# The last quarter of the final layer norm's scale and shift, moved from VectorE to GpSimd

## The reference

```python
def layer_norm(x, g, b):
    mu = jnp.mean(xf, axis=-1, keepdims=True)
    xc = xf - mu
    var = jnp.mean(xc * xc, axis=-1, keepdims=True)
    y = xc * lax.rsqrt(var + LN_EPS) * g + b
...
    x = layer_norm(DEEPNORM_ALPHA * x + y, ln_g[layer], ln_b[layer])
```

## Time and profile before

| | before |
|---|---|
| time, median of 3 runs | 3601.96 us (3601.51 to 3603.68) |
| profiled execution's span, first to last instruction | 3601.3 us |
| TensorE's last product, as the chain of waits has it | ends at 3582.83 us |
| VectorE's sixteen instructions of `ln_last` | 3586.78 to 3598.11 us |
| output issues | 4 of 512 KB, 2.8 us from issue to landing |

### The profile page before, as it was taken

One profiled execution on the slowest core, in us unless ns is written; L12 is line 12 of the kernel. 1 busy time (PEld: TensorE's weight loads), 2 busy tenths in 40 slices (PEclk: granted clock), 3 DMA queues, 4 the chain that ended last, 5 costly groups with the idle time before them and its releaser, 6 DMA issues.

```text
span 3601.3 us, 38810 instructions
## 1 busy us (share of the span) xinstructions
PE 3244.4 (90%) x13642; PEld 2303.8 (64%) x13642; DVE 1733.7 (48%) x2546; ACT 1336.4 (37%) x2042; POOL 2214.8 (61%) x1228
## 2 busy tenths in 40 slices
PE   9999999995787788777777789999999999999998
PEld 7888878883343334222322338888888888878886
DVE  7998264217666447544744552222232123435443
ACT  6776575452111001000100014444444444445653
POOL 2021767887544544555555537887788778878666
PEclk9999999997999999999999999999999999999999
DMA  7455545658999999999999985555555555555444
GB/s 229 137 151 138 170 148 161 222 176 340 419 419 420 422 419 421 421 420 422 420 416 422 419 346 195 175 172 172 169 173 174 170 168 177 172 180 177 146 145 163
DMA packets 232700, 936.78 MB, mean 260 GB/s; under 512 B 28112, under 2 KB 31184, under 8 KB 165968
## 3 DMA queue, kind: packets, MB, share of 16 engines
q0 software_dynamic: 76288, 538.74, 36.2%
q1 hardware_dynamic: 152784, 391.96, 34.3%
q10 hardware_dynamic: 3456, 3.77, 0.3%
HBM read 927.04 MB, written 2.10 MB: 258 GB/s over the span
## 4 chain that ended last, share of the span: by engine, by line
PE 54%; DMA 25%; POOL 10%; issue 5%; DVE 4%; ACT 1%; DVEq 0%; ACTq 0%; POOLq 0%; SPq 0%
PE products L665 32%; DMA arena<-peer_up_in,arena 20%; POOL weights_low L627 8%; PE products L1984 7%; PE products L1339 7%; DMA arena<-peer_down_in,arena 4%; POOL arena L1929 2%; DVE arena L1938 1%; PE products L1070 1%; PE products L2545 1%; PE products L2507 1%; PE products L1176 1%; PE products L1093 1%; PE products L1313 0%; PE products L1082 0%
## 5 line engine op out<-in xcount | busy, mean ns | idle before, releaser
L627 POOL TENSOR_TENSOR weights_low<-arena,weights_high 128x1024 fp32r<-128x1024 f32 x492 | 1208.8, 2465 | 366.2 <-ACT weights_high L615 333.4
L1984 PE MATMUL products<-arena 128*128 128x512 f32 x1984 | 940.8, 619 | 312.8 <-DMA arena<-peer_up_in,arena 230.5
L615 ACT ACTIVATE weights_high<-arena 128x1024 fp32r<-128x1024 f32 x612 | 646.3, 1059 | 991.5 <-PE products L665 965.0
L665 PE MATMUL products<-weights_high,input_high 128*128 128x512 f32 x2432 | 989.4, 407 | 1.9 <-DVE input_low L641 0.8
L665 PE MATMUL products<-weights_low,input_high 128*128 128x512 f32 x2432 | 951.2, 391 | 0.0
L665 PE MATMUL products<-weights_high,input_low 128*128 128x512 f32 x2432 | 948.9, 390 | 0.0
L1984 PEld LDWEIGHTS products<-arena 128*128 128x128 f32 x1984 | 370.3, 195 | 864.5 <-issue 453.2
L1938 DVE SCALAR_TENSOR_TENSOR arena<-arena 128x2048 f32<-128x2048 f32 x256 | 586.0, 2292 | 523.2 <-DMA arena<-peer_down_in,arena 522.8
L1929 POOL DMA_INDIRECT arena<-peer_up_in,arena x256 | 386.7, 1511 | 521.6 <-PE products L1984 497.1
L665 PEld LDWEIGHTS products<-weights_high,input_high 128*128 128x128 f32 x2432 | 457.8, 188 | 97.5 <-issue 8.0
L665 PEld LDWEIGHTS products<-weights_low,input_high 128*128 128x128 f32 x2432 | 456.8, 188 | 98.9
(11 more groups left out here) (339 smaller groups left out, 2999.4 us busy)
## 6 DMA issues: line engine op xcount, KB each, us to landing
arena<-dsa_in SPq DMA_DIRECT2D x320, 512.0 KB, 3.5
arena<-w_in_in SPq DMA_DIRECT2D x128, 512.0 KB, 4.0
arena<-mla_wide_in SPq DMA_DIRECT2D x88, 512.0 KB, 3.5
arena<-w_attn_o_in SPq DMA_DIRECT2D x32, 512.0 KB, 4.4
arena<-w_out_in SPq DMA_DIRECT2D x32, 512.0 KB, 4.7
arena<-peer_w_query_in SPq DMA_DIRECT2D x32, 512.0 KB, 4.6
arena<-dsa_w_out_in SPq DMA_DIRECT2D x32, 512.0 KB, 3.8
arena<-glu_w_b_in SPq DMA_DIRECT2D x16, 512.0 KB, 3.7
```

Source lines behind the costliest of these rows:

```text
L615: nc.scalar.activation(w_hi[:, u % RING, :, at], ring[:, u % RING, :, at], ACT.Copy).then_inc(hi_made, 1)
L627: ops.tensor_tensor(w_lo[:, u % RING, :, at], ring[:, u % RING, :, at], w_hi[:, u % RING, :, at].bitcast(F32), op=ALU.subtract).then_inc(l ...
L665: mm = nc.tensor.matmul(PS[:, bank(b) + t, 0:width], x[:, x0 + n, at], y, start=n == 0 and m == 0, stop=n == len(parts) * PK - 1 and m == 2)
L1984: mm = nc.tensor.matmul(PS[:, SUM_BANKS[q]], diag[:, d % ROWS], row[:, q * NC:(q + 1) * NC], start=h % 2 == 0 and n == 0, stop=bool(last))
```

## The change

The loop of `ln_last` goes over three quarters instead of four. The fourth is made by GpSimd in a new function behind its last `mla_lo`, with two instructions that subtract the mean and multiply by the reciprocal, a drain, two that multiply by the gain, a drain, and two that add the shift. A new semaphore, `inverse_ready`, is raised by VectorE behind `ln_inverse`; GpSimd waits for it and for the gain and shift (`ln_in`). Another, `quarter_done`, is what SyncE waits for before the fourth output.

```diff
         def ln_last(dve):
             dve.wait_ge(ln_in, 64)
-            for q in range(4):
+            for q in range(3):
...
+        def ln_last_quarter(pool):
+
+            at = slice(3 * NC, 4 * NC)
+            pool.wait_ge(ln_in, 64)
+            pool.wait_ge(inverse_ready, 1)
+            for t in range(NT):
+                nc.gpsimd.tensor_scalar(X[:, t, at], X[:, t, at], ln_moments[:, t, 0:1], full_inv[:, t:t + 1],
+                                        ALU.subtract, ALU.mult)
+            pool.drain()
+            for t in range(NT):
+                nc.gpsimd.tensor_tensor(X[:, t, at], X[:, t, at], last_gain[:, at], op=ALU.mult)
+            pool.drain()
+            for t in range(NT):
+                last = nc.gpsimd.tensor_tensor(X[:, t, at], X[:, t, at], last_shift[:, at], op=ALU.add)
+            last.then_inc(quarter_done, 1)
...
-                sp.wait_ge(ln_done, PARTS + q + 1)
+                if q < 3:
+                    sp.wait_ge(ln_done, PARTS + q + 1)
+                else:
+                    sp.wait_ge(quarter_done, 1)
...
             for n in range(len(M_ORDER)):
                 mla_lo(pool, n)
+            ln_last_quarter(pool)
...
             ln_inverse(dve, 1)
+            dve.sem_inc(inverse_ready, 1)
             ln_last(dve)
```

More of the change, by code:

```diff
@@ L581, in program @@
         normal_high, tile_made = sem("normal_high"), sem("tile_made")
+        inverse_ready, quarter_done = sem("inverse_ready"), sem("quarter_done")
         apart = {"dve": sem("apart_dve"), "pe": sem("apart_pe"), "pool": sem("apart_pool")}
```

## The result

The changed kernel takes 3609.84 us (median of 11 runs, 3607.53 to 3612.17), the kernel before 3602.31 us on the same chip (11 runs, 3599.67 to 3603.82): 1.0021 times as long, interval 1.0013 to 1.0028, or 7.5 us more. I had forecast 4.2 us more, as 3606 us. The time lies just inside the range, and 7.5 us are barely more than the 7.2 us that I had called measurable; but they are not made of the terms of my sum.

A forecast was written before the change was run, and what follows sets the result against it. Bound by VectorE's stream in series with one output DMA, the last stage was to give 3595.30 + 5.4 + 0.1 + 1.5 + 3.19 = 3605.5 us, 4.2 more than before: forecast 3606 us, range 3600.5 to 3610.

The forecast's parts named there:

- with two drains some 6.8: GpSimd's fourth quarter: its six instructions alone take 6.6 us, with two drains some 6.8, done by 3593.7.
- which nothing waits for: GpSimd's end, about 3596.3 in alternation with VectorE, holds nothing up: its output stands behind VectorE's third on SyncE's queue.
- 0.80 us from the copy: GpSimd's tensor_scalar of 512 columns, priced by scaling its 252-column copy of 396 ns; ends 0.53 and 2.66 us.
- the tensor_scalar is dear: Rival at GpSimd's fourth quarter: tensor_scalar costs more than a copy; at 2.66 us each, time 3609.8 us; chance 0.07.
- the signs that I had named: In the changed profile: VectorE's first six or so 1.2 to 2 us, third output near 3600.7, first tensor_scalar within 0.2 us.
- The 5.4 us of delay to VectorE: In `ln_last`, GpSimd's six instructions delay VectorE's three quarters by 4 x 1.05 + 2 x 0.60 us, to 3600.7.
- My 0.60 us for each tensor_scalar: In `ln_last`, each GpSimd tensor_scalar delays VectorE by 0.60 us, a pair taking 0.80 + 0.46 = 1.26.
- the four times 1.05: In `ln_last`, each of GpSimd's four two-input instructions delays VectorE by 1.05 us, a pair taking 1.71.
- the alternation of the earlier trace: Around 3270 us, VectorE's `finish_rows` and GpSimd's subtractions run in turn, 1.83 and 1.85 us each.
- The rule of the Trainium skill that I weighed: Two-SBUF-input VectorE and SBUF-reading GpSimd instructions hold shared ports for whole lengths: 7.1 us of delay, time near 3607.8.
- The 1.5 us for two outputs that stand together: At the end, the third and fourth outputs' packets follow each other: 1.5 us more than one output's tail.
- the late reload: Rival on GpSimd ahead of its fourth quarter: library reload takes the whole 36.8 us, time 3624.4 us; chance 0.08.

The follow-up runs named there:

- three quarters only: The changed kernel with the fourth quarter's scale and shift left out, GpSimd only raising `quarter_done`: 3600.15 us, 0.9994 of the kernel before.
- the early drain: The changed kernel with one more GpSimd drain, right behind its last subtraction and ahead of the library reload: 3604.36 us, 1.0005 of the kernel before.
- the two kernels of the last experiment: The changed kernel with a drain behind the row fetches and the last shift's load issued by GpSimd, as one DMA or 32: 3603.38 and 3621.95 us.

## Why the time lay in the range, and where the prediction's reasons failed

**The step that failed** is the one that gave GpSimd's stream "with two drains some 6.8" us, and the sentence built on it, that GpSimd's end is one "which nothing waits for". I had counted two drains at 0.1 us each, and at nothing in the end at 3596.3, with no row for one on GpSimd and no bound from above. The first took 7.3 us more than the work in front of it. It is the price of GpSimd's DMA issues, moved by the edit from the end of the program, where VectorE's stage hid it, into the chain. The runs show it three times over: moved to idle time it costs nothing there (the loss falls from 7.5 to 2.2 us), left out it returns at the program's end, and it comes and goes with the DMAs issued.

**The tensor_scalar was mis-sized.** I took 0.80 us from the copy between ends of 0.53 and 2.66; it is 2.09 alone, inside the ends but far from my value, and 3.09 beside VectorE, where my way gave 0.80 + 0.46 = 1.26. My rival "the tensor_scalar is dear" gave 3609.8 us, all but the time measured, but for another reason: it had VectorE delayed by 9.1 us, and VectorE ended earlier than in the forecast.

**That the time lies in the range is luck.** The forecast had VectorE last, at 3600.7 - 3586.7 = 14.0 us behind the reciprocal, and GpSimd done at 9.6; measured, VectorE was done at 9.1 and GpSimd came last, at 18.9. Of the signs that I had named, only the start of the first tensor_scalar came (0.22 us behind the reciprocal); VectorE's first instructions did not last 1.2 to 2 us, and the fourth output did wait for GpSimd. A delay of VectorE that did not come and a drain that I had all but left out led, by two different paths, to ends of the span within 4 us of each other, and the range's upper end came from the dear tensor_scalar, which would have lengthened the time by another path.

GpSimd's end, from the forecast's 9.6 us behind the reciprocal to 18.9: 6.19 - 2 x 1.26 = 3.7 us for the tensor_scalars, 7.5 for the drains, less 4 x 1.71 - 2 x 2.48 = 1.9 for two-input instructions that ran alone.

**The ports.** The 5.4 us of delay to VectorE were 9.12 - 8.65 = 0.5 us in the changed kernel (8.65 with three quarters only), because ten of VectorE's twelve instructions ran at 0.74 to 0.75 us, those beside the tensor_scalars too but for two (0.94 and 1.02, in the merged rows of 1.60 and 1.68 us), and the two-input ones came too late to meet it. My 0.60 us for each tensor_scalar was thus too much, and the four times 1.05 were right in kind: with the early drain the alternation of the earlier trace rows came, a pair every 1.6 us where I had 1.71, and VectorE lost 12.0 - 9.1 = 2.9 us. These fell on three of its instructions, of 1.60 to 1.75 us instead of 0.74: 0.95 each, so near my 1.05 where the two really meet. The rule of the Trainium skill that I weighed ("SBUF — State Buffer", section "Who interferes with whom"), whole instructions in turn, doesn't fit the tensor_scalars: VectorE finished four of its instructions while one of GpSimd's went on.

**The output's tail.** The 1.5 us for two outputs that stand together are right where they do: 1.4 us with three quarters only. In the changed kernel the fourth came 9.8 us after the third, so the term was nothing, and from GpSimd's end to the span's end are 22.1 - 18.9 = 3.2 us, as taken over from before.

**What held.** The raise of `inverse_ready` costs nothing to speak of (the first of `ln_last` starts 0.12 us behind the reciprocal, 0.09 before). The reload is hidden, and the late reload with it is out: the first tensor_scalar starts 0.22 us behind the reciprocal. With the early drain the reload could begin only behind it, at 3582.95, and the tensor_scalar still started at 3585.55, so it takes at most 2.6 us here; the 6 us of the Trainium skill ("GPSIMD Engine Reference", section 2.1) aren't seen, and the first tensor_scalar lasts 3.12 us, the second 3.07. A quarter is worth 2.8 us of VectorE, but only 1.4 us of the span, since the outputs then queue.

## What to carry to other kernels

Where an engine gets new work at its end, look at what that engine's final drain did before: if it outlasts the last instruction by microseconds, as here by 7.3, a drain that the edit puts on the path may have to pay for it, and a drain put earlier into idle time took it away here. Before work moves from VectorE to GpSimd, see whether VectorE reads a second input from SBUF at that time: here the 2.8 us taken off VectorE came back as 3.3 us of delay (12.0 with the early drain against 8.7 with three quarters only), until that input lay in PSUM. And at a kernel's tail the order in which outputs become ready is part of the sum: a free helper for a quarter brought 1.4 us of 2.8, until its output went ahead of the last one.

## What the runs showed of the hardware that I had not expected

A drain on GpSimd costs some 0.08 us for each DMA that GpSimd itself has issued since its last drain (1, 32 and 80 plain DMAs: 0.1, 2.6 and 6.6 us), 7.3 us behind 512 indirect ones, and that they have landed long before, or that the engine has been idle for 10 us, doesn't spare it. With transfers under way it lasts longer, to 4.1 us behind the last packet of the fetches. Between 80 and 512 no run was made, so where the upper end lies is open, and what the drain does in that time too.

On GpSimd a tensor_scalar with two operations is dearer (2.1 us for 512 columns) than a two-input product (1.25), and in the changed kernel it left VectorE nearly undisturbed but was itself drawn out by half, to 3.1 us. These are no fixed prices: in the two kernels of the last experiment, where VectorE's first instruction starts 0.20 us behind the reciprocal instead of 0.13, the tensor_scalars take 2.6 us each, and two of VectorE's instructions beside them 1.17 instead of 0.75. The two-input instruction, the cheaper one, is the one that holds VectorE up most, 0.95 us each time.
